# A four-layer trunk on one core: 16 unused columns between the high and the low parts of x and of h

## The chip, the cores and the metric

The kernel runs on one core of a Trainium2 chip. The metric is the time of one execution on the device in microseconds (us). The kernel before was run three times: 2007.51, 2009.39 and 2010.02 us, median 2009.39 us. The run that was profiled took 2008.11 us, and its span, from the first to the last recorded instruction, is 2006.3 us.

## The reference

A residual trunk of four layers over 256 tokens of width 1024, all in float32. Each layer is a half-weighted SwiGLU feed-forward block (FFN), a mixer, and a second FFN; the mixers are a forgetting attention (layers 0 and 3), a causal convolution module (layer 1) and a differential attention (layer 2).

```python
def _swiglu(h, w_gate, w_up, w_down):
    return (jax.nn.silu(h @ w_gate) * (h @ w_up)) @ w_down

for i in range(DEPTH):
    x = x + 0.5 * _swiglu(_rms_norm(x, norm_ffn1[i]), ffn1_w_gate[i], ffn1_w_up[i], ffn1_w_down[i])
    h = _rms_norm(x, norm_mix[i])
    ...                      # y = the layer's mixer of h
    x = x + y
    x = x + 0.5 * _swiglu(_rms_norm(x, norm_ffn2[i]), ffn2_w_gate[i], ffn2_w_up[i], ffn2_w_down[i])
```

D_FF is 2816, so an FFN holds three matrices of 1024 x 2816 values. The eight FFNs are most of the work.

## The kernel before

**Split operands.** Every large product is made from float32 values that are split in two: a high part (the value rounded to the type float32r, by ScalarE) and a low part (what is left, by VectorE). The product is high*high + high*low + low*high, accumulated in PSUM. For the weights the parts are `w_high` and `w_low`; for the activations they are `x_high` and `x_low`, the two halves of one tensor `x_both` with the shape [128, 2, 8, 256], and for the FFN's hidden values the halves of `h_both`, [128, 2, 22, 256]. A tile of one part is 256 columns of 4 bytes, 1024 bytes in each partition.

**Blocks.** The weights stream in as 332 blocks (`load`), a ring of 5 slots of 2048 columns. `split_high` (L470) and `split_low` (L788) split each. TensorE then works through a block.

**The FFN on TensorE.** `tile`, inside `ffn`, makes one PSUM bank from one block and one half of its 256 output columns (n is 0 or 1), over eight tiles k of x. `down` does the same with tiles of h: its blocks c=0 and c=1 have eight tiles k, its block c=2 has six. Both call `both_parts` (the function is in the listing below), which issues two kinds of matmul:
- `on_both` (L1364): the stationary operand is `w_high`, the moving operand is 512 columns, 256 of the high part and then 256 of the low part of the same tile k. One instruction makes high*high in the left half of the bank and high*low in the right half.
- `on_high` (L1369): the stationary operand is `w_low`, the moving operand is the 256 columns of the high part.

For each bank the order is one `on_both`, eight `on_high`, seven `on_both` (six and six in the blocks c=2). Every matmul has a weight load of its own (LDWEIGHTS of 128 columns), which is read while the matmul before it runs.

**The mixers.** They use `three_passes` (L1355, L1356, L1357): three matmuls of 256 columns for each product, one per pair of parts, through `columns_half` (x moves), `tokens_half` (the weights move and x is stationary) and `rows_block` (the parts `o_high` and `o_low` of the mixer's output move).

**Where things lie.** The tensors are placed one behind another in SBUF in the order of the code. In the compiled kernel the weight slots start 128 bytes past a multiple of 1024 bytes, `x_high` and `x_low` 192 bytes past one, both parts of h 64 bytes past one, and both parts of o 224 bytes past one. `shift_x` (64 bytes) and `shift_h` (800 bytes) are unused tensors ahead of `x_both` and `h_both`. The low part of x starts 8192 bytes behind its high part, that of h 22528 bytes behind; both distances are multiples of 1024.

**What sets the order.** It is written out by hand for each engine, with semaphores between the engines. No scheduler takes part.

Of the kernel before, what the change touches and what calls it, by code (L numbers as in the profile page):

```python
# [7 lines left out]
F32R = mybir.dt.float32r  # L8
# [6 lines left out]
P = 128  # L15
DEPTH = 4
SEQ = 256
D = 1024
KT = D // P
# [16 lines left out]
FF_TILES = D_FF // P  # L36
# [22 lines left out]
def build_trunk(nc, A, out):  # L59
# [12 lines left out]
    with ExitStack() as ctx:  # L72
        def sb(name, shape, dt=F32):
            return ctx.enter_context(nc.sbuf_tensor("sb_" + name, shape, dt))
# [11 lines left out]
        xT = sb("xT", [P, KT, SEQ])  # L86
        x_square = sb("x_square", [P, KT, SEQ])
        sb("shift_x", [P, 16])
        x_both = sb("x_both", [P, 2, KT, SEQ], F32R)
        x_high, x_low = x_both[:, 0, :, :], x_both[:, 1, :, :]  # L90
        square_sum = sb("square_sum", [P, SEQ])
        square_pair = sb("square_pair", [P, SEQ])
# [65 lines left out]

        sb("shift_h", [P, 200])
        with ExitStack() as during_ffn:  # L160
            h_both = during_ffn.enter_context(nc.sbuf_tensor("sb_h_both", [P, 2, FF_TILES, SEQ], F32R))
            gate_part = during_ffn.enter_context(nc.sbuf_tensor("sb_gate_part", [P, 2, SEQ], F32))
            up_part = during_ffn.enter_context(nc.sbuf_tensor("sb_up_part", [P, 2, SEQ], F32))
        with ExitStack() as during_taps:
# [1696 lines left out]
```

## Time and profile before

| | before |
|---|---|
| runs | 2007.51, 2009.39, 2010.02 us |
| profiled execution | 2008.11 us |
| its span | 2006.3 us |
| TensorE matmul busy | 1960.5 us (98%), 12584 matmuls |
| weight loads busy | 1722.1 us (86%) |
| VectorE busy | 1424.5 us (71%) |
| ScalarE busy | 1045.4 us (52%) |
| GpSimd busy | 114.2 us (6%) |
| granted TensorE clock, mean | 0.997 |

A matmul's record is longer than its turn in the pipeline: the records of successive matmuls overlap. The time that one costs is read from the starts, as the distance between the start of a group of matmuls and the start of the next group, divided by the number in the group. The column "mean ns of one" does not give it.

### The profile page before, as it was taken

What the parts mean: (1) busy time and instruction counts of PE and PEld (TensorE: products, weight loads), DVE (VectorE), ACT (ScalarE), POOL (GpSimd) and SP (SyncE); (2) the same over time, 40 slices, a digit from 0 to 9 for tenths busy, and PEclk for the clock granted to TensorE, in tenths of its full rate; (3) what the DMA queues carried; (4) which work ended last, traced back from release to release, by engine and by line L of the source; (5) the groups of instructions that cost most, each with busy time, mean ns of one, the idle gap of its engine ahead of it and who ended that gap; (6) DMA issues with size and microseconds to landing.
All of it is one profiled execution on the core that took longest, in us unless ns stands there. A gap on an engine that the chain in (4) does not pass through costs nothing.

```text
span 2006.3 us, 29077 instructions
## 1 busy us (share of the span) xinstructions
PE 1960.5 (98%) x12584; PEld 1722.1 (86%) x12584; DVE 1424.5 (71%) x1631; ACT 1045.4 (52%) x1247; POOL 114.2 (6%) x120
## 2 busy tenths in 40 slices
PE   7999999999999998999999999999999999999999
PEld 6888788888888896988888888888888888788887
DVE  7776777876787564777587658887658765778763
ACT  5544556654554344654465455565446545456542
POOL 2000201000200001100000000010010001101000
PEclk9999999999999999999999999999999999999999
DMA  7655433665665583565666553356566655335553
GB/s 225 196 186 180 147 127 116 200 194 182 194 193 190 182 253 83 184 194 185 196 190 195 176 182 126 109 184 190 179 200 189 189 187 171 126 113 182 189 184 110
DMA packets 336365, 350.14 MB, mean 175 GB/s; under 512 B 10077, under 2 KB 331886, under 8 KB 336238
## 3 DMA queue, kind: packets, MB, share of 16 engines
q1 hardware_dynamic: 331742, 343.58, 54.1%
q10 hardware_dynamic: 4496, 4.70, 1.0%
q8 instruction: 99, 1.62, 0.3%
q14 instruction: 28, 0.23, 0.0%
HBM read 346.04 MB, written 2.22 MB: 174 GB/s over the span
## 4 chain that ended last, share of the span: by engine, by line
PE 88%; DVE 5%; ACT 4%; issue 2%; DMA 1%; POOL 1%; ACTq 0%; DVEq 0%; POOLq 0%
PE banks L1364 48%; PE banks L1369 24%; PE banks L1355 4%; PE banks L1357 4%; PE banks L1356 4%; ACT sb_w_high L470 1%; DVE sb_w_low L788 1%; ACT sb_scores L596 1%; PE banks L1567 1%; PE banks L1797 1%; DVE sb_neg_max L1055 1%; PE banks L1605 0%; PE banks L1716 0%; DVE sb_scores L1048 0%; DMA u_away<-sb_u_pad 0%
## 5 line engine op out<-in xcount | busy, mean ns | idle before, releaser
L788 DVE TENSOR_TENSOR sb_w_low<-sb_raw,sb_w_high 128x2048 fp32r<-128x2048 f32 (+1 forms) x332 | 753.6, 2274 | 236.5 <-ACT sb_w_high L470 235.6
L1364 PE MATMUL banks<-sb_x_both,sb_w_high 128*128 128x512 f32 x2816 | 723.0, 392 | 3.5 <-DVE sb_w_low L788 3.5
L470 ACT ACTIVATE sb_w_high<-sb_raw 128x2048 fp32r<-128x2048 f32 (+1 forms) x332 | 619.1, 1869 | 140.1 <-DMA sb_raw<-in_ffn_w_down 111.1
L1364 PEld LDWEIGHTS banks<-sb_x_both,sb_w_high 128*128 128x128 f32 x2816 | 497.7, 188 | 82.9 <-DVE sb_w_low L788 3.9
L1369 PEld LDWEIGHTS banks<-sb_x_both,sb_w_low 128*128 128x128 f32 x2816 | 391.2, 188 | 36.8
L1369 PE MATMUL banks<-sb_x_both,sb_w_low 128*128 128x256 f32 x2816 | 399.5, 278 | 0.0
L1364 PE MATMUL banks<-sb_h_both,sb_w_high 128*128 128x512 f32 x1408 | 360.1, 394 | 0.0
L1364 PEld LDWEIGHTS banks<-sb_h_both,sb_w_high 128*128 128x128 f32 x1408 | 250.2, 188 | 45.7
L1369 PEld LDWEIGHTS banks<-sb_h_both,sb_w_low 128*128 128x128 f32 x1408 | 190.8, 188 | 17.1
L1369 PE MATMUL banks<-sb_h_both,sb_w_low 128*128 128x256 f32 x1408 | 194.3, 279 | 0.0
L488 ACT ACTIVATE sb_x_both<-sb_xT,sb_vec 128x256 fp32r<-128x256 f32 x96 | 43.5, 501 | 202.6 <-DVE sb_xT L821 174.0
L1355 PE MATMUL banks<-sb_x_both,sb_w_high 128*128 128x256 f32 x512 | 146.7, 286 | 0.0
L541 ACT ACTIVATE sb_up_part<-banks 128x512 f32<-128x512 f32 x88 | 52.4, 595 | 175.0 <-PE banks L1364 175.0
L1357 PE MATMUL banks<-sb_x_both,sb_w_low 128*128 128x256 f32 x512 | 142.8, 279 | 0.0
L1356 PE MATMUL banks<-sb_x_both,sb_w_high 128*128 128x256 f32 x512 | 142.7, 279 | 0.0
L541 ACT ACTIVATE sb_gate_part<-banks 128x512 f32<-128x512 f32 x88 | 52.3, 594 | 163.1 <-PE banks L1364 163.1
L954 DVE TENSOR_TENSOR sb_up_part<-banks,sb_up_part 128x512 f32<-128x512 f32 x88 | 60.6, 689 | 59.1 <-ACT sb_up_part L541 59.1
L1355 PEld LDWEIGHTS banks<-sb_x_both,sb_w_high 128*128 128x128 f32 x512 | 96.1, 188 | 3.2 <-issue 3.0
L1356 PEld LDWEIGHTS banks<-sb_x_both,sb_w_high 128*128 128x128 f32 x512 | 96.2, 188 | 1.7 <-issue 1.4
L938 DVE TENSOR_TENSOR sb_gate_part<-banks,sb_gate_part 128x512 f32<-128x512 f32 x88 | 60.7, 690 | 50.6 <-ACT sb_gate_part L541 50.3
L1357 PEld LDWEIGHTS banks<-sb_x_both,sb_w_low 128*128 128x128 f32 x512 | 96.0, 188 | 0.0
L818 DVE SCALAR_TENSOR_TENSOR sb_xT<-banks,sb_xT 128x512 f32<-128x512 f32 x32 | 22.1, 691 | 95.3 <-PE banks L1364 95.3
(210 smaller groups left out, 1950.5 us busy)
## 6 DMA issues: line engine op xcount, KB each, us to landing
sb_raw<-in_ffn_w_gate SPq DMA_DIRECT2D x88, 1024.0 KB, 5.4
sb_raw<-in_ffn_w_up SPq DMA_DIRECT2D x88, 1024.0 KB, 5.4
sb_raw<-in_ffn_w_down SPq DMA_DIRECT2D x64, 1024.0 KB, 5.0
sb_raw<-in_ffn_w_down SPq DMA_DIRECT2D x32, 768.0 KB, 4.3
sb_raw<-in_fox_w_in SPq DMA_DIRECT2D x24, 1024.0 KB, 5.3
sb_raw<-in_conv_w_pw SPq DMA_DIRECT2D x12, 1024.0 KB, 5.3
sb_raw<-in_diff_w_in SPq DMA_DIRECT2D x12, 1024.0 KB, 5.0
sb_raw<-in_fox_w_out SPq DMA_DIRECT2D x8, 1024.0 KB, 4.9
```

Source lines behind the costliest of these rows:

```text
L470: act.activation(slot(w_high, b)[:, 0:width(b)], slot(raw, b)[:, 0:width(b)], ACT.Copy).then_inc(S["high_ready"], 1)
L488: act.activation(x_high[:, t, :], xT[:, t, :], ACT.Copy, scale=vec[:, col + t:col + t + 1]).then_inc(S["xhigh_ready"], 1)
L541: act.activation((up_part if which else gate_part)[:, :, :], banks[:, at:at + 2, SEQ:], ACT.Copy).then_inc(S["up_part_ready" if which else ...
L788: dve.tensor_tensor(slot(w_low, b)[:, 0:width(b)], slot(raw, b)[:, 0:width(b)], slot(w_high, b)[:, 0:width(b)].bitcast(F32), ALU.subtract) ...
L818: dve.scalar_tensor_tensor(xT[:, 2 * T:2 * T + 2, :], sums[:, :, SEQ:], 0.5, xT[:, 2 * T:2 * T + 2, :], ALU.mult, ALU.add).then_inc(S["x_h ...
L938: dve.tensor_tensor(gate_part[:, :, :], banks[:, at:at + 2, 0:SEQ], gate_part[:, :, :], ALU.add).then_inc(S["gate_sum_ready"], 1)
L954: dve.tensor_tensor(up_part[:, :, :], banks[:, at:at + 2, 0:SEQ], up_part[:, :, :], ALU.add).then_inc(S["up_sum_ready"], 1)
L1355: pe.matmul(dst, s_high, m_high, start=first, stop=False, skip_group_check=loose)
L1356: pe.matmul(dst, s_high, m_low, start=False, stop=False, skip_group_check=loose)
L1357: return pe.matmul(dst, s_low, m_high, start=False, stop=last, skip_group_check=loose)
L1364: return pe.matmul(pair(bank[at][:, :]), high[:, n * P:(n + 1) * P], m_both, start=first, stop=last, skip_group_check=True)
L1369: pe.matmul(bank[at][:, SEQ:2 * SEQ], low[:, n * P:(n + 1) * P], m_high, start=False, stop=False, skip_group_check=True)
```

## The change

`x_both` and `h_both` become views of tensors whose two parts are each 16 columns (64 bytes) longer than the tiles need. Nothing reads or writes those columns.

```diff
-        x_both = sb("x_both", [P, 2, KT, SEQ], F32R)
+        x_parts = sb("x_both", [P, 2, KT * SEQ + 16], F32R)
+        x_both = x_parts[:, :, 0:KT * SEQ].rearrange("p a (k n) -> p a k n", n=SEQ)
         x_high, x_low = x_both[:, 0, :, :], x_both[:, 1, :, :]
...
-            h_both = during_ffn.enter_context(nc.sbuf_tensor("sb_h_both", [P, 2, FF_TILES, SEQ], F32R))
+            h_parts = during_ffn.enter_context(nc.sbuf_tensor("sb_h_both", [P, 2, FF_TILES * SEQ + 16], F32R))
+            h_both = h_parts[:, :, 0:FF_TILES * SEQ].rearrange("p a (k n) -> p a k n", n=SEQ)
```

Each engine issues the same instructions in the same order as before. Only addresses differ. `x_low` lies 64 bytes further on. The tensor has grown by 128 bytes, since both parts have the 16 columns, so everything behind it lies 128 bytes further on, `h_both` and o among them, and the low part of h 192 bytes further on. The starts past a multiple of 1024 bytes are then:

| tensor | before | after |
|---|---|---|
| weight slots | 128 | 128 |
| x_high | 192 | 192 |
| x_low | 192 | 256 |
| h high part | 64 | 192 |
| h low part | 64 | 256 |
| o_high, o_low | 224 | 352 |

## Rows read from the trace of the kernel before

**Rows 1.** The page: busy time, share of the span and instructions of each engine.

```profile
PE 1960.5 (98%) x12584; PEld 1722.1 (86%) x12584; DVE 1424.5 (71%) x1631; ACT 1045.4 (52%) x1247; POOL 114.2 (6%) x120
```

**Rows 2.** The page: the chain of work that ended last, share of the span by line.

```profile
PE banks L1364 48%; PE banks L1369 24%; PE banks L1355 4%; PE banks L1357 4%; PE banks L1356 4%; ACT sb_w_high L470 1%; DVE sb_w_low L788 1%; ACT sb_scores L596 1%; PE banks L1567 1%; PE banks L1797 1%; DVE sb_neg_max L1055 1%; PE banks L1605 0%; PE banks L1716 0%; DVE sb_scores L1048 0%; DMA u_away<-sb_u_pad 0%
```

**Rows 3.** Busy time by stretch, one FFN; the first row names the columns.

```profile
core 0: us, PE busy (x) PEld busy (x) DVE busy (x) ACT busy (x) POOL busy (x), PEclk, DMA share, GB/s
338.00:521.00 183.00, 183.00 (x1060) 160.54 (x1059) 132.68 (x125) 95.32 (x96) 7.97 (x11) 1.00 0.60 189
```

**Rows 4.** Groups of matmuls, whole span: busy us, mean ns | idle before.

```profile
L1364 PE MATMUL banks<-sb_x_both,sb_w_high 128*128 128x512 f32 x2816 | 723.0, 392 | 3.5 <-DVE sb_w_low L788 3.5
L1369 PE MATMUL banks<-sb_x_both,sb_w_low 128*128 128x256 f32 x2816 | 399.5, 278 | 0.0
L1364 PE MATMUL banks<-sb_h_both,sb_w_high 128*128 128x512 f32 x1408 | 360.1, 394 | 0.0
L1369 PE MATMUL banks<-sb_h_both,sb_w_low 128*128 128x256 f32 x1408 | 194.3, 279 | 0.0
L1355 PE MATMUL banks<-sb_x_both,sb_w_high 128*128 128x256 f32 x512 | 146.7, 286 | 0.0
...
L1355 PE MATMUL banks<-sb_o_high,sb_w_high 128*128 128x256 f32 x256 | 75.5, 295 | 6.3 <-DVE sb_o_low L1300 5.6 <-DVE sb_o_low L1108 0.8
...
L1355 PE MATMUL banks<-sb_w_high,sb_x_both 128*128 128x256 f32 x192 | 64.2, 334 | 0.0
...
L1716 PE MATMUL banks<-sb_xT,sb_gate_w_gained 128*16 128x256 f32 x32 | 7.3, 380 | 0.0
```

**Rows 5.** TensorE in order of time, tiles of x: start us, us, the group.

```profile
421.49 1.11 PE L1369 MATMUL banks<-sb_x_both,sb_w_low 128*128 128x256 f32 x8
...
424.27 1.07 PE L1369 MATMUL banks<-sb_x_both,sb_w_low 128*128 128x256 f32 x8
425.17 1.99 PE L1364 MATMUL banks<-sb_x_both,sb_w_high 128*128 128x512 f32 x8
427.00 1.11 PE L1369 MATMUL banks<-sb_x_both,sb_w_low 128*128 128x256 f32 x8
427.94 2.00 PE L1364 MATMUL banks<-sb_x_both,sb_w_high 128*128 128x512 f32 x8
...
443.54 1.11 PE L1369 MATMUL banks<-sb_x_both,sb_w_low 128*128 128x256 f32 x8
```

**Rows 6.** The same for tiles of h, T=1 of `down`.

```profile
475.39 1.10 PE L1369 MATMUL banks<-sb_h_both,sb_w_low 128*128 128x256 f32 x8
476.33 2.03 PE L1364 MATMUL banks<-sb_h_both,sb_w_high 128*128 128x512 f32 x8
478.20 1.08 PE L1369 MATMUL banks<-sb_h_both,sb_w_low 128*128 128x256 f32 x8
479.12 1.79 PE L1364 MATMUL banks<-sb_h_both,sb_w_high 128*128 128x512 f32 x7
...
490.72 1.10 PE L1369 MATMUL banks<-sb_h_both,sb_w_low 128*128 128x256 f32 x8
```

**Rows 7.** The same for x moving in three passes, layer 0.

```profile
226.92 0.28 PE L1355 MATMUL banks<-sb_x_both,sb_w_high 128*128 128x256 f32 x1
...
231.00 0.28 PE L1355 MATMUL banks<-sb_x_both,sb_w_high 128*128 128x256 f32 x1
```

**Rows 8.** The same for x moving in three passes, layer 3.

```profile
1714.33 0.28 PE L1355 MATMUL banks<-sb_x_both,sb_w_high 128*128 128x256 f32 x1
...
1716.45 0.28 PE L1355 MATMUL banks<-sb_x_both,sb_w_high 128*128 128x256 f32 x1
```

**Rows 9.** The same for o moving in three passes, layer 0.

```profile
319.94 0.28 PE L1355 MATMUL banks<-sb_o_high,sb_w_high 128*128 128x256 f32 x1
...
322.10 0.28 PE L1355 MATMUL banks<-sb_o_high,sb_w_high 128*128 128x256 f32 x1
```

**Rows 10.** The same for sixteen matmuls of plain float32, layer 0.

```profile
209.98 3.63 PE L1716 MATMUL banks<-sb_xT,sb_gate_w_gained 128*16 128x256 f32 x16
```

## The prediction

> **What bounds the kernel now.** I read the page's busy times first. TensorE is busy for 1960.5 of 2006.3 us, VectorE for 71% of the span, ScalarE for 52% [rows 1]. The chain of waits says the same by line: 48% of the span is the 512-column matmul `on_both`, 24% the 256-column matmul `on_high`, 12% the three passes of the mixers [rows 2]. The busy times by stretch then show an FFN: 183.00 us of matmul in 183.00 us, the clock granted in full, VectorE at 132.68 us and the DMA engines at a share of 0.60 [rows 3]. In the whole span the four groups of FFN matmuls have 3.5 us of idle time before them [rows 4]. So in the eight FFNs nothing but the pace of TensorE's own stream sets the end, and a nanosecond on each of many thousand matmuls arrives at the end in full. Other engines have about 50 us of slack in each FFN.
>
> The last view is TensorE in order of time, from which the pace is read as distance between starts. For x, 64 `on_both` and 64 `on_high` go from 421.49 to 443.54 us: 22.05 / 64 = 344.5 ns for one of each [rows 5]. For h, 44 and 44 go from 475.39 to 490.72 us: 15.33 / 44 = 348.4 ns [rows 6]. The same instructions on the same kinds of shapes differ by 3.9 ns. Within x, eight `on_high` take 0.90 us with n=1 (425.17 - 424.27), 113 ns each, but 0.94 us with n=0 (427.94 - 427.00), 117.5 ns each; eight `on_both` between them take 1.83 us, 229 ns each [rows 5]. With h, eight `on_both` take 1.87 us, 234 ns each (478.20 - 476.33) [rows 6]. The three passes show two paces for one piece of code: 36 matmuls in 4.08 us, 113.3 ns, in layer 0 [rows 7], and 18 in 2.12 us, 117.8 ns, in layer 3 [rows 8]. With o, whose tiles start 32 bytes off a multiple of 64, 18 take 2.16 us, 120.0 ns [rows 9]. The pace thus sits on a few levels, and which level it takes goes with the place of the moving tile, the place of the weights (n), and the state in which the stream arrives (rows 7 against 8).
>
> **Removed and added instructions: none.** Issue order, waits, DMAs and queues stay, so no wait and no queue needs costing. Extra SBUF is 256 bytes. The moved buffers of VectorE, ScalarE and GpSimd keep their lengths and multiples of 32 bytes. I cost their move at nothing: VectorE's slack of 50 us per FFN hides it, and without that cover 1% on its 132.68 us would be 1.3 us per FFN.
>
> The Trainium skill speaks against any effect of addresses. "SBUF — State Buffer", section Who interferes with whom, says that PE never waits on another engine, and "TensorE: Matmul & The Clock Gate", section Back-to-back issue gap, gives a warm gap of N/2.4 + 2.5 ns, which is 109.2 ns for 256 columns and 215.8 ns for 512. By that rule the pace would not know the address and the change would be worth zero. The trace disagrees in the numbers: 113 to 120 and 229 to 234 ns [rows 5 to 9].
>
> **h, high part moved by 128 bytes.** It comes to start 192 bytes past a multiple of 1024, exactly where x_high starts now. If its place is what makes h slower than x, each pair of matmuls of h goes from 348.4 to 344.5 ns: 1408 [rows 4] x 3.9 ns = 5.5 us less.
>
> **Low parts 64 bytes further.** Now the low part starts a whole multiple of 1024 bytes behind its high part, and after the change 64 bytes more; inside each `on_both` the moving read jumps there after 256 columns. The trace shows no matmul with such a jump, so I bound it. Below: plain float32 with 16 stationary columns keeps (3.63 - 0.38) / 15 = 216.7 ns for a matmul [rows 4, 10]; were that reached by an `on_both`, x would gain 229 - 217 = 12 ns x 2816 = 34 us and h 17 x 1408 = 24 us. Above: o's place costs 120.0 - 113.3 = 6.7 ns per 256 columns [rows 7, 9]; on one of the two parts that is 6.7 x 4224 = 28 us. The nearest rows are those of x and h themselves, whose levels are 4.4 ns apart in most steps (113.3 to 117.8, 229 to 234) [rows 5 to 8]. I take zero for the jump, since both x and h stay on 64-byte places, and keep one level up or down, 4.4 x 4224 = 18.6 us, for the range.
>
> **The other 256-column matmuls.** `on_high` reads high parts only. For x nothing moves; for h it comes to x's place, where the paces are already alike (0.94 us for eight at 475.39, 0.92 at 478.20) [rows 6]. The three passes of x are 3 x 512 matmuls and those with x stationary 3 x 192 [rows 4]; half of them changing level either way is 2112 / 2 x 4.4 ns = 4.6 us, sign unknown. o keeps its 32-byte offset, so its 120.0 ns for 3 x 256 matmuls stands. I take zero and leave 5 us each way.
>
> **Sum.** -5.5 us on the profiled 2008.11 us gives 2002.6. The median of the runs is 1.28 us above the profiled one, so I forecast 2003.9 us.
>
> **Rivals.**
> - *No effect.* The difference between x and h comes from something the change leaves alone, for instance the sequence in which the stream enters a tile, and the addresses in steps of 64 bytes do nothing. For it: the three passes change pace between layers with identical addresses [rows 7, 8]. Against it: n=0 and n=1 of x differ tile after tile with nothing else different [rows 5]. Time 2009.4. This is also what the two pages would give.
> - *Slower: the broken run.* High part, low part, and the next tile's high part now start at the same place within 1024 bytes, so the moving read goes round any pattern of that length without a skip. Afterwards `on_both` skips 64 bytes of it at the low part, and at its end the next tile begins on the place just read. The place is the jump inside `on_both` and the one behind it; if the read stalls once per instruction, the price is one level, 4.4 ns x 4224 = 18.6 us. With the gain of h against it, 13 us slower: 2022.5. It decides from a stall of 1.3 ns per `on_both` on (5.5 / 4224), which eats the gain. For it: an `on_both` costs 229 ns, 2.4 more than two fast `on_high` of 113.3, so a jump already isn't free. Against it: o, h and x carry their own offsets and no row shows a skip costing anything.
> - *Much faster.* The equal places of high and low are themselves what costs. Then the 64 bytes take one level off each `on_both`, 18.6 us, and h's 5.5 come on top: 24 us, 1985.3. For it: both kinds of `on_both` are 12 to 17 ns above the plain float32 pace [rows 5, 6, 10]. Against it: the fast level of 256 columns, with no jump in it, is already 113.3, so two of them make 227, and a gain of more than 2 ns for x has to come from somewhere else.
> - *The change does not do what it says.* It does: the layout moves as listed. No chance is given to it.
>
> **Chances.** Forecast (h gains 3 to 9 us with the rest about even) 0.34; no effect 0.22; slower 0.28; much faster 0.16. A measurement of this kernel tells about 0.2%, 4 us, from no change. Of the forecast 0.28 is beyond 4 us faster and 0.06 within; of "no effect" 0.17 is within, and the 5 us of the three passes put 0.02 on the faster side and 0.03 on the slower; "slower" leaves 0.01 within. So faster 0.28 + 0.16 + 0.02 = 0.46, within 0.06 + 0.17 + 0.01 = 0.24, slower 0.27 + 0.03 = 0.30. The likeliest case has a range of 1998 to 2008. The range of all reaches to the two far cases, with their far halves left out: 1988 to 2023.
>
> **What would show it right or wrong.** In the changed profile, groups of eight `on_both` on h at 1.83 us from start to start instead of 1.87, and those on x unchanged at 1.83, show the forecast. `on_both` at 1.87 us or more on x shows the broken run; at 1.80 or less the much faster case. FFNs shorter or longer than 183.0 us by the same amount each would show that all of it is TensorE's pace; idle time before L1364 beyond the 3.5 us would show a wait that I do not expect. The prediction is wrong if the jump to the low part moves the pace at all, since I put it at zero, or if h at x's place keeps its 348 ns.

## The result: 21.6 us slower, and the profile after

The changed kernel takes 2030.45 us (median of four runs, 2029.31 to 2031.38), the kernel before 2008.86 us beside it. The ratio is 1.011, with an interval of 1.0096 to 1.0124. The forecast was 2003.9 us, with a range of 1988 to 2023. The forecast missed in direction, and the time lies outside the range. Interrupted executions (one of the ten of `x_gap_512`, at 8502.97 us, and three of the kernel before in the later sets, at 3257.72 to 6910.65 us) count in no ratio below, but do count in the medians given.

The page after, with its busy times and the chain by line. The functions stand two lines further down, so `on_both` is L1366 and `on_high` L1371:

```profile
PE 1984.9 (98%) x12584; PEld 1731.9 (85%) x12584; DVE 1425.0 (70%) x1631; ACT 1045.2 (51%) x1247; POOL 115.9 (6%) x120
...
PE banks L1366 48%; PE banks L1371 24%; PE banks L1357 4%; PE banks L1358 4%; PE banks L1359 4%; ACT sb_w_high L472 1%; DVE sb_w_low L790 1%; ACT sb_scores L598 1%; PE banks L1569 1%; PE banks L1799 1%; DVE sb_neg_max L1057 0%; PE banks L1607 0%; PE banks L1718 0%; DVE sb_scores L1050 0%; PE banks L1590 0%
```

Against [rows 1, 2], TensorE is busy for 24.4 us more, VectorE for 0.5, and the shares of the chain are the same. One FFN-long stretch of the changed kernel, busy times as in [rows 3]:

```profile
core 0: us, PE busy (x) PEld busy (x) DVE busy (x) ACT busy (x) POOL busy (x), PEclk, DMA share, GB/s
338.00:521.00 183.00, 183.00 (x1056) 159.64 (x1055) 134.76 (x131) 98.06 (x102) 9.72 (x12) 1.00 0.59 186
```

TensorE still never pauses, but it does 1056 matmuls in those 183 us where it did 1060. The four groups of FFN matmuls, as in [rows 4]:

```profile
L1366 PE MATMUL banks<-sb_x_both,sb_w_high 128*128 128x512 f32 x2816 | 735.6, 396 | 3.5 <-DVE sb_w_low L790 3.5
L1371 PE MATMUL banks<-sb_x_both,sb_w_low 128*128 128x256 f32 x2816 | 405.5, 280 | 0.0
L1366 PE MATMUL banks<-sb_h_both,sb_w_high 128*128 128x512 f32 x1408 | 360.8, 395 | 0.0
L1371 PE MATMUL banks<-sb_h_both,sb_w_low 128*128 128x256 f32 x1408 | 197.4, 280 | 0.0
```

Counts and idle time before them are unchanged. So no wait came in: the same matmuls follow one another more slowly. The starts tell how much. First the tiles of x, to be laid beside [rows 5]:

```profile
424.27 1.10 PE L1371 MATMUL banks<-sb_x_both,sb_w_low 128*128 128x256 f32 x8
425.22 2.03 PE L1366 MATMUL banks<-sb_x_both,sb_w_high 128*128 128x512 f32 x8
427.08 1.11 PE L1371 MATMUL banks<-sb_x_both,sb_w_low 128*128 128x256 f32 x8
428.03 2.03 PE L1366 MATMUL banks<-sb_x_both,sb_w_high 128*128 128x512 f32 x8
...
452.38 1.10 PE L1371 MATMUL banks<-sb_x_both,sb_w_low 128*128 128x256 f32 x8
```

From 424.27 to 452.38 us lie ten tiles, 80 `on_both` and 80 `on_high`: 28.11 / 80 = 351.4 ns for one of each, where it was 344.5. Eight `on_high` now take 0.95 us in either half (it was 0.90 with n=1), eight `on_both` 1.86 instead of 1.83. Then the tiles of h, beside [rows 6]:

```profile
471.81 1.10 PE L1371 MATMUL banks<-sb_h_both,sb_w_low 128*128 128x256 f32 x8
472.76 2.03 PE L1366 MATMUL banks<-sb_h_both,sb_w_high 128*128 128x512 f32 x8
...
487.27 1.10 PE L1371 MATMUL banks<-sb_h_both,sb_w_low 128*128 128x256 f32 x8
```

Here 15.46 / 44 = 351.4 ns, where it was 348.4. x and h now have the same pace. The sum: 2816 x 6.9 ns = 19.4 us for x and 1408 x 3.0 ns = 4.2 us for h, together 23.6 us, and the two profiled spans differ by 2029.6 - 2006.3 = 23.3 us.

### The profile page after: what moved, and what is told of

The parts are those of the page before. It is cut to its first block, busy times and chain, and to the rows that moved or that the text cites. A ratio compares the mean times of both kernels' runs of the same rounds, so it can differ in the third digit from the quotient of the medians.

```text
span 2029.6 us, 29077 instructions
## 1 busy us (share of the span) xinstructions
PE 1984.9 (98%) x12584; PEld 1731.9 (85%) x12584; DVE 1425.0 (70%) x1631; ACT 1045.2 (51%) x1247; POOL 115.9 (6%) x120
## 4 chain that ended last, share of the span: by engine, by line
PE 88%; DVE 5%; ACT 4%; issue 2%; DMA 1%; POOL 1%; ACTq 0%; DVEq 0%; POOLq 0%
PE banks L1366 48%; PE banks L1371 24%; PE banks L1357 4%; PE banks L1358 4%; PE banks L1359 4%; ACT sb_w_high L472 1%; DVE sb_w_low L790 1%; ACT sb_scores L598 1%; PE banks L1569 1%; PE banks L1799 1%; DVE sb_neg_max L1057 0%; PE banks L1607 0%; PE banks L1718 0%; DVE sb_scores L1050 0%; PE banks L1590 0%
## 5 line engine op out<-in xcount | busy, mean ns | idle before, releaser
L1366 PE MATMUL banks<-sb_x_both,sb_w_high 128*128 128x512 f32 x2816 | 735.6, 396 | 3.5 <-DVE sb_w_low L790 3.5
L1366 PEld LDWEIGHTS banks<-sb_x_both,sb_w_high 128*128 128x128 f32 x2816 | 498.7, 188 | 92.3 <-DVE sb_w_low L790 3.9
L1371 PEld LDWEIGHTS banks<-sb_x_both,sb_w_low 128*128 128x128 f32 x2816 | 395.5, 188 | 40.5
L1371 PE MATMUL banks<-sb_x_both,sb_w_low 128*128 128x256 f32 x2816 | 405.5, 280 | 0.0
L1366 PE MATMUL banks<-sb_h_both,sb_w_high 128*128 128x512 f32 x1408 | 360.8, 395 | 0.0
L1366 PEld LDWEIGHTS banks<-sb_h_both,sb_w_high 128*128 128x128 f32 x1408 | 250.6, 187 | 47.0
L1371 PEld LDWEIGHTS banks<-sb_h_both,sb_w_low 128*128 128x128 f32 x1408 | 192.4, 188 | 17.3
L1371 PE MATMUL banks<-sb_h_both,sb_w_low 128*128 128x256 f32 x1408 | 197.4, 280 | 0.0
L1359 PE MATMUL banks<-sb_x_both,sb_w_low 128*128 128x256 f32 x512 | 144.3, 282 | 0.0
```

The source lines that it names most:

```text
L1359: return pe.matmul(dst, s_low, m_high, start=False, stop=last, skip_group_check=loose)
L1366: return pe.matmul(pair(bank[at][:, :]), high[:, n * P:(n + 1) * P], m_both, start=first, stop=last, skip_group_check=True)
L1371: pe.matmul(bank[at][:, SEQ:2 * SEQ], low[:, n * P:(n + 1) * P], m_high, start=False, stop=False, skip_group_check=True)
```

## The experiments

"Place" below is where a tile starts, counted in bytes from where the weight slots start, modulo 256 (why 256 comes out of the second and third set). Before, x has its high and low part at places 64 and 64, h at 192 and 192, o at 96 and 96. After, x has 64 and 128, h 64 and 128, o 224 and 224. "Pair" is the time of one `on_both` and one `on_high`, read from starts as above. The rows of the experiments stand where a verdict rests on them.

**Which part of the change costs.** Four kernels ran beside a kernel before at 2006.92 us.

`x_gap_only`:

```diff
-        x_both = sb("x_both", [P, 2, KT, SEQ], F32R)
+        x_parts = sb("x_both", [P, 2, KT * SEQ + 16], F32R)
+        x_both = x_parts[:, :, 0:KT * SEQ].rearrange("p a (k n) -> p a k n", n=SEQ)
...
-        sb("shift_h", [P, 200])
+        sb("shift_h", [P, 168])
```

> Only x's low part moves, by 64 bytes; h and o are put back to where they were before (shift_h 168 columns instead of 200). Theory A (the jump from high to low inside on_both is no longer a multiple of 1024 bytes): x's on_both at 233.6 ns instead of 229.2 (2816 x 4.4 = 12.4 us) and its on_high with n=1 at 117.8 instead of 113.9 (1408 x 3.9 = 5.5 us), so about 18 us slower than before, 2027. Theory B (the loss comes from h's or o's new places, and x only inherits it): under 5 us slower, 2009 to 2014.

Measured 2025.43 us, ratio 1.0089 (1.0074 to 1.0104): 18.5 us of the loss, as theory A had it. Nine tiles of x:

```profile
422.39 1.10 PE L1370 MATMUL banks<-sb_x_both,sb_w_low 128*128 128x256 f32 x8
...
447.68 1.11 PE L1370 MATMUL banks<-sb_x_both,sb_w_low 128*128 128x256 f32 x8
```

25.29 / 72 = 351.3 ns. The gap in x alone gives x its whole loss. The tensors between `x_both` and `h_both` lie 128 bytes further on in this kernel as well; in `x_moved_64` they move by only 64, and the loss is the same.

`h_gap_only`: the same gap in `h_both` alone, nothing else.

```diff
+            h_parts = during_ffn.enter_context(nc.sbuf_tensor("sb_h_both", [P, 2, FF_TILES * SEQ + 16], F32R))
+            h_both = h_parts[:, :, 0:FF_TILES * SEQ].rearrange("p a (k n) -> p a k n", n=SEQ)
```

> Only h's low part moves, by 64 bytes; x, o and h's high part stay. Theory A: on_both of h is at 233.4 ns already, so it stays or rises by one level at most (1408 x 4.4 = 6 us); on_high of h goes to 117.8 everywhere (704 x 4 + about 200 x 4 = 3.6 us): 2012 to 2019. Theory B (h's high part at 192 is what costs): no change, 2009.

Measured 2007.33 us, ratio 0.9999 (0.999 to 1.0008). No loss. A gap of the same 64 bytes that costs x 18 us costs h nothing, which speaks against theory A: h's pair is even a little shorter.

```profile
475.19 1.08 PE L1370 MATMUL banks<-sb_h_both,sb_w_low 128*128 128x256 f32 x8
...
490.44 1.08 PE L1370 MATMUL banks<-sb_h_both,sb_w_low 128*128 128x256 f32 x8
```

15.25 / 44 = 346.6 ns against 348.4 [rows 6].

`x_gap_1024`: x's low part 1024 bytes further, the gap filled by a tensor that is needed anyway.

```diff
-        x_both = sb("x_both", [P, 2, KT, SEQ], F32R)
+        with ExitStack() as apart:
+            x_parts = apart.enter_context(nc.sbuf_tensor("sb_x_both", [P, 2, KT * SEQ + 256], F32R))
+        x_both = x_parts[:, :, 0:KT * SEQ].rearrange("p a (k n) -> p a k n", n=SEQ)
+        sb("x_high_place", [P, KT * SEQ])
+        square_sum = sb("square_sum", [P, SEQ])
+        sb("x_low_place", [P, KT * SEQ])
...
-        square_sum = sb("square_sum", [P, SEQ])
```

> x's low part lies 1024 bytes further on instead of 64; square_sum fills the gap, and everything behind it stays in place. Theory A (only what is left over after a multiple of 1024 bytes counts): the pace of before, x's on_both 229.2 ns, 2009 us. Rival (the distance of exactly 8192 bytes is what was good, any other costs): x as in x_gap_only, about 2027 us.

Measured 2007.63 us, ratio 1.0003 (0.9994 to 1.0012). A distance of 9216 bytes is as good as 8192.

`x_moved_64`: no gap, both parts of x 64 bytes further.

```diff
-        sb("shift_x", [P, 16])
+        sb("shift_x", [P, 32])
...
-        sb("shift_h", [P, 200])
+        sb("shift_h", [P, 184])
```

> Both parts of x move by 64 bytes together, h and o stay. Theory A (the jump counts, not the place): the pace of before, 2009 us. Theory C (the place of the low part against the weights' place, 128 bytes past it, is what costs): x's on_both at 233.6 ns, 2021 to 2027 us. If the high part's place counts for on_high too, it goes to 117.8 ns for both n.

Measured 2025.45 us, ratio 1.0086 (1.007 to 1.0103). This is the run on which theory A fell: the distance is a multiple of 1024, the read takes no odd jump, and the loss is the same 18.5 us.

```profile
422.63 1.10 PE L1369 MATMUL banks<-sb_x_both,sb_w_low 128*128 128x256 f32 x8
...
447.92 1.12 PE L1369 MATMUL banks<-sb_x_both,sb_w_low 128*128 128x256 f32 x8
```

25.29 / 72 = 351.3 ns again.

**Place against what.** The second four ran beside a kernel before at 2007.49 us.

`all_moved_64`:

```diff
+        sb("shift_all", [P, 16])
         with ExitStack() as landing:
```

> 64 unused bytes ahead of everything: weights, x, h and o all move by 64 bytes, their places against each other stay. Theory C (the place against the weights counts): the pace of before on every group, 2007 to 2010 us. Theory D (the absolute place counts, 256 bytes past a multiple of 1024 is slow for x): x's on_both at 233 ns, on_high at 118, about 18 us slower, 2025.

Measured 2007.53 us, ratio 0.9997 (0.9987 to 1.0006). x now lies at the absolute addresses that `x_moved_64` gave it, and costs nothing. It is the place against the weight slots that counts.

`h_at_x_place`:

```diff
-        sb("shift_h", [P, 200])
+        sb("shift_h", [P, 232])
```

> Both parts of h move by 128 bytes to 192 past a multiple of 1024, the place that x has; o moves by 128 as well. This is the term of the prediction by itself. Theory P (the prediction's): h's pair goes from 348.4 to 344.5 ns, 5.5 us faster, 2002. Rival (x and h differ by something other than place): no change, 2007 to 2009.

Measured 2004.21 us, ratio 0.9984 (0.9975 to 0.9994): 3.3 us faster. With h at places 64 and 64 eight `on_both` take 1.84 us (477.37 - 475.53), where they took 1.87 [rows 6]:

```profile
474.59 1.10 PE L1369 MATMUL banks<-sb_h_both,sb_w_low 128*128 128x256 f32 x8
475.53 2.00 PE L1364 MATMUL banks<-sb_h_both,sb_w_high 128*128 128x512 f32 x8
477.37 1.11 PE L1369 MATMUL banks<-sb_h_both,sb_w_low 128*128 128x256 f32 x8
...
479.92 1.11 PE L1369 MATMUL banks<-sb_h_both,sb_w_low 128*128 128x256 f32 x8
...
489.85 1.07 PE L1369 MATMUL banks<-sb_h_both,sb_w_low 128*128 128x256 f32 x8
...
495.13 1.11 PE L1369 MATMUL banks<-sb_h_both,sb_w_low 128*128 128x256 f32 x8
```

From 474.59 to 489.85 us lie 44 pairs, and from 479.92 to 495.13 another 44: 15.26 and 15.21 us, mean 346.3 ns a pair, 2.1 less than before. 1408 x 2.1 = 3.0 us. The 3.3 us are not h's alone: o has moved to place 224 in this kernel, as in the changed one, and its passes are a little shorter there (the rows stand with `h_and_o_placed`).

`x_high_back`, x's high part at place 0, its low part at 64:

```diff
-        sb("shift_x", [P, 16])
-        x_both = sb("x_both", [P, 2, KT, SEQ], F32R)
+        pass
+        x_parts = sb("x_both", [P, 2, KT * SEQ + 16], F32R)
...
-        sb("shift_h", [P, 200])
+        sb("shift_h", [P, 184])
```

> x's high part moves 64 bytes back (to 128, level with the weights), its low part stays at 192: the distance between the parts is that of the change, 8256 bytes. Theory C1 (the low part's place is what counts for on_both): on_both at 229 ns, on_high perhaps changed, 2000 to 2015. Theory C2 (the distance of 8256 counts together with the place): on_both at 233 ns, about 18 us slower, 2025.

Measured 2033.75 us, ratio 1.0129 (1.0114 to 1.0144), the slowest of all. The low part lies where it was good, so its place alone (C1) is refuted; the high part's place costs as well, and both kinds of matmul read the high part. C2 is not borne out in size either: the loss is 26.3 us where it had 18.

`x_low_back`, a gap of 240 columns as in `x_gap_1024`, places 64 and 0:

```diff
+            x_parts = apart.enter_context(nc.sbuf_tensor("sb_x_both", [P, 2, KT * SEQ + 240], F32R))
...
+        sb("x_high_place", [P, KT * SEQ])
+        gate_w = sb("gate_w", [P, KT, FOX_HEADS])
+        sb("x_gap_rest", [P, 112])
+        sb("x_low_place", [P, KT * SEQ])
...
-        gate_w = sb("gate_w", [P, KT, FOX_HEADS])
...
-        sb("shift_h", [P, 200])
+        sb("shift_h", [P, 88])
```

> x's high part stays at 192, its low part comes to lie 64 bytes nearer in place (128 past a multiple of 1024, level with the weights; 9152 bytes behind the high part). Theory C1 (a low part further from the weights is slow, a nearer one is not): 229 ns or less for on_both, 2000 to 2009 us. Theory C2 (only equal places of high and low are fast): 233 ns, 2025 us.

Measured 2023.79 us, ratio 1.008 (1.0065 to 1.0095). A low part nearer to the weights is slow too, as C2 had it. C2's general form, that only equal places are fast, does not hold for h: its unequal places 192 and 0 (`h_gap_only`) were no slower than 192 and 192.

**The weight load's read, and the period.** The third four ran beside a kernel before at 2008.69 us.

`one_weight` and `one_weight_gap`: in the layouts of before and of after, each FFN weight load reads the same value 128 times.

```diff
-                return pe.matmul(pair(bank[at][:, :]), high[:, n * P:(n + 1) * P], m_both,
+                return pe.matmul(pair(bank[at][:, :]), high[:, n * P:n * P + 1].broadcast_to([P, P]), m_both,
...
-                pe.matmul(bank[at][:, SEQ:2 * SEQ], low[:, n * P:(n + 1) * P], m_high,
+                pe.matmul(bank[at][:, SEQ:2 * SEQ], low[:, n * P:n * P + 1].broadcast_to([P, P]), m_high,
```

> The layout of before; every weight load of the FFNs reads one value per partition 128 times instead of 128 values in a row (the FFN's products are therefore other ones; 8448 matmuls and 8448 loads stay). Theory E (the moving read is held up where it meets the weight load's read, which runs through 512 bytes at the same time): the step pattern changes; on_both and on_high fall to one level, the fast one or below: on_high 109 to 113 ns for both n, on_both 216 to 227 ns; 30 us or more faster, under 1980. Theory M (the moving read alone sets the pace): 229 and 113 to 118 as before, 2007.

> The same with the layout of after. Theory E: within 3 us of one_weight, the gap costs nothing once the weight load stands still. Theory M: 21 us slower than one_weight, as after against before.

Measured 2009.95 and 2013.17 us, ratios 1.0004 (0.9995 to 1.0014) and 1.0021 (1.0012 to 1.0031). The gap costs 3.2 us here and 21.6 us with the true weight loads; the mixers' weight loads are the true ones in both kernels. Two rows of each kernel, tiles of x:

```profile
422.15 1.08 PE L1369 MATMUL banks<-sb_x_both,sb_w_low 128*128 128x256 f32 x8
...
449.82 0.40 PE L1369 MATMUL banks<-sb_x_both,sb_w_low 128*128 128x256 f32 x2
```

```profile
422.36 1.08 PE L1371 MATMUL banks<-sb_x_both,sb_w_low 128*128 128x256 f32 x8
...
447.30 1.09 PE L1371 MATMUL banks<-sb_x_both,sb_w_low 128*128 128x256 f32 x8
```

27.67 / 80 = 345.9 ns and 24.94 / 72 = 346.4 ns. Theory M, in which the moving read alone sets the pace, is refuted: only the addresses that the weight loads read differ from before and after, and most of the gap's price is gone. What ScalarE, VectorE and the DMAs write into the weight slots is the same as before and after, so a collision of the moving read with those writes alone does not explain the gap's price. Theory E was right that the two reads bear on each other, and wrong on the size: it expected a gain of 30 us once the weight load stands still, and there was none. A load that reads one address again and again is no cheaper than a walking one at a good place.

`x_moved_256`, and `x_gap_512`, which has a gap as in `x_gap_1024` with the 128 columns of `gate_w` in it:

```diff
-        sb("shift_x", [P, 16])
+        sb("shift_x", [P, 80])
...
-        sb("shift_h", [P, 200])
+        sb("shift_h", [P, 136])
```

```diff
+            x_parts = apart.enter_context(nc.sbuf_tensor("sb_x_both", [P, 2, KT * SEQ + 128], F32R))
...
+        sb("x_high_place", [P, KT * SEQ])
+        gate_w = sb("gate_w", [P, KT, FOX_HEADS])
+        sb("x_low_place", [P, KT * SEQ])
...
-        gate_w = sb("gate_w", [P, KT, FOX_HEADS])
```

> Both parts of x 256 bytes further (place 448, 320 past the weights' place); h and o stay. If the pattern of places repeats every 256 bytes or less: 229 ns for on_both, 2007 us. If it repeats every 512 or 1024 bytes: another level, 233 ns as for the other places tried, 2020 to 2030, or a new one.

> x's low part 512 bytes further (8704 behind the high part), high part in place. If the pattern repeats every 512 bytes or less: 229 ns, 2007 us. If only every 1024: on_both at 232 to 234 ns, 2020 to 2027 us.

Measured 2007.73 us, ratio 0.9996 (0.9987 to 1.0006), and 2009.54 us, ratio 1.0001 (0.9992 to 1.0011). Moves by 256, 512 and 1024 bytes are all free. The pattern repeats every 256 bytes or a part of that.

**The rule tried on new places.** The last four ran beside a kernel before at 2008.57 us.

`x_gap_128`, as `x_gap_only` but:

```diff
+        x_parts = sb("x_both", [P, 2, KT * SEQ + 32], F32R)
...
-        sb("shift_h", [P, 200])
+        sb("shift_h", [P, 136])
```

> x's low part 128 bytes further (32 unused columns), high part, h and o in place. Rule so far (only 64 past the weights, modulo 256, is fast): low part at 192 past them, on_both at 232 to 234 ns, 2020 to 2027 us. If the pattern repeats every 128 bytes: 229 ns, 2008 us.

Measured 2021.47 us, ratio 1.0062 (1.0048 to 1.0076). The period is not 128.

`weights_moved_64`, in which only the weight slots, `xT` and `x_square` move:

```diff
+        sb("shift_all", [P, 16])
         with ExitStack() as landing:
...
-        sb("shift_x", [P, 16])
+        pass
```

> Only the weight slots (and the float32 x beside them) move by 64 bytes; x_both, h and o stay where they were, so x is level with the weights and h 128 bytes from them. If the distance to the weights counts: h at 232 to 234 ns for on_both and 119 for on_high (as x at that distance in x_moved_64), x at a level not seen yet for both parts, 230 to 236 ns: 2015 to 2035 us. If the absolute place counts: 2008 us.

Measured 2025.87 us, ratio 1.0086 (1.0072 to 1.01), with not one byte of x, h or o at another address. The tiles of h:

```profile
479.10 1.13 PE L1370 MATMUL banks<-sb_h_both,sb_w_low 128*128 128x256 f32 x8
...
494.59 1.11 PE L1370 MATMUL banks<-sb_h_both,sb_w_low 128*128 128x256 f32 x8
```

15.49 / 44 = 352.0 ns at places 128 and 128, which x had in `x_moved_64` with 351.3.

`gap_of_64_columns`, against the changed kernel:

```diff
-        x_parts = sb("x_both", [P, 2, KT * SEQ + 16], F32R)
+        x_parts = sb("x_both", [P, 2, KT * SEQ + 64], F32R)
...
-            h_parts = during_ffn.enter_context(nc.sbuf_tensor("sb_h_both", [P, 2, FF_TILES * SEQ + 16], F32R))
+            h_parts = during_ffn.enter_context(nc.sbuf_tensor("sb_h_both", [P, 2, FF_TILES * SEQ + 64], F32R))
```

> The change itself with 64 unused columns (256 bytes) instead of 16 in each part, so that every place is the old one modulo 256. If only the place modulo 256 counts: 2008 us, 229 ns. If the gap as such costs: 2025 to 2030 us.

Measured 2006.74 us, ratio 0.9996 (0.9987 to 1.0005). A gap as such is free.

`h_and_o_placed`: no gap, the three operands at place 64.

```diff
-        sb("shift_h", [P, 200])
+        sb("shift_h", [P, 168])
...
+        sb("shift_o", [P, 24])
         o_high = sb("o_high", [P, KT, SEQ], F32R)
```

> h 128 bytes back and o 32 bytes back, so that x, h and o all start 64 bytes behind the weights' place, counted in a pattern of 256 bytes; no gaps. If the place within 256 bytes is all that counts: h's on_both at 229 ns (as in h_at_x_place), o's three passes at 117 instead of 119.9 ns (768 x 2.9 = 2.2 us): 2008 - 5 - 2 = 2001. If h_at_x_place gained by something else: no change.

Measured 2003.65 us, ratio 0.9976 (0.9966 to 0.9985): 4.9 us faster than before, where 7 were expected; by the two ratios it is 1.3% below the changed kernel. h's pair reads as in `h_at_x_place`. The passes of o, beside [rows 9]:

```profile
319.40 0.28 PE L1356 MATMUL banks<-sb_o_high,sb_w_high 128*128 128x256 f32 x1
...
322.58 0.28 PE L1356 MATMUL banks<-sb_o_high,sb_w_high 128*128 128x256 f32 x1
```

27 matmuls in 3.18 us, 117.8 ns instead of 120.0. Two other traces have o at places that are also 32 bytes off a multiple of 64. First the changed kernel (place 224), then `weights_moved_64` (place 32):

```profile
322.84 0.28 PE L1357 MATMUL banks<-sb_o_high,sb_w_high 128*128 128x256 f32 x1
...
326.75 0.28 PE L1357 MATMUL banks<-sb_o_high,sb_w_high 128*128 128x256 f32 x1
```

```profile
321.00 0.28 PE L1356 MATMUL banks<-sb_o_high,sb_w_high 128*128 128x256 f32 x1
...
325.56 0.28 PE L1356 MATMUL banks<-sb_o_high,sb_w_high 128*128 128x256 f32 x1
```

33 matmuls in 3.91 us are 118.5 ns, and 39 in 4.56 us are 116.9 ns. So the 32 bytes are not what makes o slow before; place 96 is the slowest of the four.

What all of it gives for a pair, in ns, with h in the rows where it was measured:

| places of high and low part | x | h |
|---|---|---|
| 64, 64 | 344.5 (before) | 346.3 (h_at_x_place) |
| 192, 0 | | 346.6 (h_gap_only) |
| 192, 192 | | 348.4 (before) |
| 64, 192 | 349.1 (x_gap_128) | |
| 0, 0 | 349.1 (weights_moved_64) | |
| 64, 0 | 350.0 (x_low_back) | |
| 64, 128 | 351.3 (x_gap_only) | 351.4 (after) |
| 128, 128 | 351.3 (x_moved_64) | 352.0 (weights_moved_64) |
| 0, 64 | 353.4 (x_high_back) | |

The figures that no row above shows are read in the same way: `x_gap_128` 27.93 us for 80 pairs, `weights_moved_64` 27.93 for 80, `x_low_back` 28.00 for 80, `x_high_back` 28.27 for 80.

## Why the prediction was wrong

**What bounds the kernel: right.** TensorE's own pace sets the end. All of the 23.3 us came through it and no wait appeared, as the tests at the prediction's end asked.

**Pace on levels that go with the place: right, and underused.** The prediction read from [rows 5 to 9] that the place of the moving tile against the weights goes with the level. It then asked only what the change does to h's high part. One piece of its evidence does not fit the rule that the runs gave: it put the two paces of `on_high` on x (0.90 and 0.94 us for eight) down to the place of the weights, n=0 against n=1. Those lie 512 bytes apart, two whole patterns, so their place modulo 256 is the same. What makes x's groups alternate is not shown.

**The low parts' move at zero: the step that failed.** The prediction took zero "since both x and h stay on 64-byte places". That reason does not hold: 64 bytes are a quarter of the pattern's 256. Measured, x's low part at place 128 costs 18.5 us by itself (`x_gap_only`). A part of that lies in `on_high`, which does not read the low part at all: in the change its busy time on x went from 399.5 [rows 4] to 405.5 us, that of `on_both` from 723.0 to 735.6. In the starts of the whole trace, 157 of the 320 groups of eight `on_high` on x that stand apart took 0.90 us before, the others 0.94; in `x_gap_only` 7 take 0.90. So the matmuls took the slower of two paces that were there before. I read this as a state in which the stream enters the group, as between [rows 7] and [rows 8]; how it is carried over is not shown. The prediction took `on_high` of x as untouched because its addresses were.

**h at x's place: right in kind, and lost in the change.** Without the gap, the move is worth 3.3 us where 5.5 were forecast (`h_at_x_place`), and a part of that may be o's; h's pair comes down to 346.3 ns and not to x's 344.5, so 2.1 of the 3.9 ns arrive. By the starts of the whole trace h's `on_both` comes down from 232.6 to 229.3 ns, close to x's 228.7, but its `on_high` goes up from 115.9 to 116.7, as more of its groups take 0.94 us. The prediction had put `on_high` of h at nothing. In the change it never arrives, since h's low part moved on to place 128 with it, and h ended 3.0 ns a pair slower.

**o at 120.0 ns: wrong in a small term.** The prediction let o's pace stand because o keeps its 32-byte offset. In the change it came to 118.5 ns, 768 x 1.5 = 1.2 us less.

**The rivals.** "The broken run" gave 2022.5 us, 8 short, with a mechanism that the runs refute: it put the price on the odd jump between the parts, and `x_moved_64` pays it without such a jump while `h_gap_only` and `gap_of_64_columns` jump free. Its price, one level on each of 4224 `on_both`, 18.6 us, was near the 21.6 only in sum: by the groups' busy times x's `on_both` paid 12.6 us and h's 0.7, where it had 12.4 and 6.2, and `on_high`, for which it had nothing, paid 9.1. "No effect" is refuted, and the Trainium skill with it at this point: in "TensorE: Matmul & The Clock Gate", section Step-by-step: what each phase is for, it states that loading the next weights does not take SBUF read bandwidth from the running matmul, since the two have ports of their own. For these float32r matmuls the runs disagree: `weights_moved_64` lost 17.3 us with x, h and o in place, and `one_weight_gap` took most of the gap's price away by changing nothing but the addresses that the weight loads read. "Much faster" is refuted too: the fastest pair of places found, 64 and 64, is an equal one, and no unequal pair that was tried is faster.

**The range.** It ended at 2023 because the high bound was one level per `on_both`, with h's gain against it. What `on_high` lost (6.0 us on x, where nothing that it reads had moved, and 197.4 - 194.3 = 3.1 us on h, whose high part had, by the groups' busy times) was not in it.

**Open.** Why place 64 is the best of those tried, how the two reads hold each other up, and how a pace carries over to the next group, is not shown. For x and h only steps of 64 bytes were tried, and not all pairs of places. All runs are of float32r matmuls with a weight load each.

## What to carry to other kernels

Where TensorE streams float32r matmuls back to back, each with a weight load of its own, the distance between moving and stationary operands in SBUF, modulo 256 bytes, is a tuning knob worth 1.5% here (2003.65 to 2033.75 us). Any padding in front of one of them turns it, also padding that was added for something else; so hold the places fixed by a compensating shift when a layout changes, and try all four steps of 64 bytes for every operand. Read the effect from starts of groups in the trace: a record is longer than its turn (396 ns where a turn is 233), and its length is no measure of the pace.

## What the runs showed of the hardware that was not expected

- The pace of a matmul depends on the place of its operands against each other, with a pattern of 256 bytes: 344.5 to 353.4 ns for the same pair of instructions. Moving everything by 64 bytes changes nothing (2007.53 us), moving only the weight slots, `xT` and `x_square` costs 17.3 us.
- The level carries over: `on_high` of x got slower from a move of data that it does not read: in `x_gap_only` nearly all its groups of eight take 0.94 us, before half of them took 0.90.
- A weight load that reads one address 128 times makes the layout nearly indifferent (3.2 us for the gap instead of 21.6) without making anything faster (2009.95 us).
- o's matmuls of 256 columns take 120.0 ns at place 96, 118.5 at 224, 117.8 at 64 and 116.9 at 32. Being 32 bytes off a multiple of 64 is not what slows them.
